# Modulation rows in six groups: one ahead of layer 0, five between its projections, in 32-column strips

## The reference

```python
def _modulation(cond, w, b):
    return jnp.split(jax.nn.silu(cond) @ w + b, N_MOD, axis=-1)      # N_MOD = 6, D = 1024
...
for l in range(DEPTH):                                               # DEPTH = 2
    sh1, sc1, g1, sh2, sc2, g2 = _modulation(c[:, None, :], ada_w[l], ada_b[l])
    csh1, csc1, cg1, csh2, csc2, cg2 = _modulation(c_ctx[None, None, :], ada_w[l], ada_b[l])
    ux = x * (1.0 + sc1) + sh1
    uc = ctx * (1.0 + csc1) + csh1
    yx, yc = _hybrid_mixer(ux, uc, w_in[l], ...)          # input projection first
    x = _layer_norm(DEEPNORM_ALPHA * x + g1 * yx, ...)
    fx = _peer(x * (1.0 + sc2) + sh2, ...)
    x = _layer_norm(DEEPNORM_ALPHA * x + g2 * fx, ...)    # ctx likewise, in layer 0
```

## Time and profile before

| | us |
|---|---|
| median of 3 runs (4849.0 to 4859.0) | 4858.26 |
| the profiled execution's span | 4851.8 |
| prologue, to the first transpose of X | 189.84 |
| of it PE in the 384 modulation matmul records | 166.6 |
| projections of layer 0, from there to the barrier | about 286 |
| PE busy over the span | 4056.9 (84%) |

### The profile page before, as it was taken

One profiled execution on the slowest core, in us unless ns is written; L12 is line 12 of the kernel. 1 busy time (PEld: TensorE's weight loads), 2 busy tenths in 40 slices (PEclk: granted clock), 3 DMA queues, 4 the chain that ended last, 5 costly groups with the idle time before them and its releaser, 6 DMA issues.

```text
span 4851.8 us, 47489 instructions
## 1 busy us (share of the span) xinstructions
PE 4056.9 (84%) x11304; PEld 1920.3 (40%) x11304; DVE 3217.5 (66%) x8492; ACT 843.4 (17%) x2182; POOL 1502.4 (31%) x1349
## 2 busy tenths in 40 slices
PE   8999899687887887887888879989788788788887
PEld 1354675333333333333333324456433333333332
DVE  0220864787777887787787863065588787778776
ACT  0100341111111111111111111023111111111111
POOL 0000010344443443443444430001144344344443
PEclk9999799999999999999999999989899999999999
DMA  9411112999998998998999982122499899899998
GB/s 325 161 52 50 66 63 77 365 416 404 376 417 364 420 414 341 411 418 337 420 418 385 416 334 72 38 98 83 170 411 419 343 414 413 335 418 416 391 412 355
DMA packets 260491, 1484.23 MB, mean 306 GB/s; under 512 B 23943, under 2 KB 48775, under 8 KB 95767
## 3 DMA queue, kind: packets, MB, share of 16 engines
q0 software_dynamic: 184320, 1342.26, 67.3%
q1 hardware_dynamic: 76060, 140.67, 8.5%
HBM read 1476.40 MB, written 2.24 MB: 305 GB/s over the span
## 4 chain that ended last, share of the span: by engine, by line
PE 51%; DVE 26%; issue 15%; DMA 6%; DVEq 2%; ACT 1%; POOL 0%; SPq 0%; POOLq 0%; ACTq 0%
PE ps L723 22%; PE ps L715 6%; DMA arena<-in_updown,arena 5%; PE ps L565 4%; DVE arena L1312 3%; DVE arena L1305 3%; PE ps L522 3%; PE ps L580 3%; PE ps L683 3%; PE ps L585 2%; DVE arena L1275 1%; PE ps L652 1%; DVE arena L1280 1%; DVE arena L1278 1%; PE ps L608 1%
## 5 line engine op out<-in xcount | busy, mean ns | idle before, releaser
L723 PE MATMUL ps<-arena 128*128 128x512 f32 x5120 | 2433.3, 620 | 537.8 <-DVE arena L1305 534.7
L976 POOL DMA_INDIRECT arena<-in_updown,arena x1280 | 1461.4, 1142 | 2225.6 <-PE ps L723 1717.8
L723 PEld LDWEIGHTS ps<-arena 128*128 128x128 f32 x5120 | 938.2, 194 | 2000.5 <-DVE arena L1305 1157.6
L1312 DVE CUSTOM_DVE_ANT_0 arena<-arena 128x1024 bf16<-128x1024 f32 x1280 | 1563.2, 1221 | 173.5 <-DMA arena<-in_updown,arena 107.5
L920 ACT ACTIVATE arena<-arena 128x1 f32<-128x1 f32 x1280 | 252.2, 202 | 2726.3 <-DVE arena L1312 2688.5
L1305 DVE TENSOR_SCALAR arena<-CN,arena 128x128 f32<-128x128 f32 x1280 | 440.9, 344 | 85.6 <-ACT arena L920 46.7
L963 POOL TENSOR_TENSOR arena<-arena 128x256 f32<-128x256 f32 x64 | 40.7, 667 | 1092.9 <-DMA arena<-in_bias 1092.9
L715 PE MATMUL ps<-arena 128*128 (+1 forms) x1280 | 302.4, 391 | 2.3 <-ACT arena L936 2.3
L1237 DVE MAX8 arena<-ps 128x8 f32<-128x128 f32 x80 | 24.0, 299 | 388.4 <-PE ps L715 388.2
L715 PEld LDWEIGHTS ps<-arena 128*128 128x128 f32 x1280 | 252.7, 198 | 68.5 <-issue 32.5
L565 PE MATMUL ps<-arena 128*128 128x512 f32 (+1 forms) x672 | 233.5, 508 | 0.0
(11 more groups left out here) (184 smaller groups left out, 2894.6 us busy)
## 6 DMA issues: line engine op xcount, KB each, us to landing
arena<-in_ada_w SPq DMA_DIRECT2D x24, 2048.0 KB, 7.9
arena<-in_updown,arena POOLq DMA_INDIRECT x1280
arena<-in_wq SPq DMA_DIRECT2D x32, 512.0 KB, 4.3
arena<-in_w_in SPq DMA_DIRECT2D x6, 2048.0 KB, 8.8
arena<-in_w_in SPq DMA_DIRECT2D x24, 512.0 KB, 3.8
arena<-in_bias SPq DMA_DIRECT2D x16, 512.0 KB, 3.6
arena<-in_w_out SPq DMA_DIRECT2D x2, 4096.0 KB, 13.4
arena<-negm_rows SPq DMA_DIRECT2D x16, 384.0 KB, 4.4
```

What stands on the lines that cost most here:

```text
L723: mm = e.matmul(ps[hf][:], diag[:, k % 2, :], ring[:, k % RING, D + hf * 512:D + (hf + 1) * 512], start=False, stop=False, skip_group_chec ...
L976: e.indirect_dma_start(ring[:, k % RING, :], None, updown, bass.IndirectOffsetOnAxis(ap=idx16[:, k:k + 1], axis=0)).then_inc(sem(f"rows{k ...
L1312: e.tensor_tensor_reduce(prod[:, k % 2, :], ring[:, k % RING, 0:D], u, 1.0, 0.0, ALU.mult, ALU.add, dots[:, k:k + 1]).then_inc(sem("L.dot_ ...
```

## The change

The 12288 columns become six groups of 2048. A group is multiplied as four pieces of 512 columns whose results go to partitions 0, 32, 64 and 96 of one PSUM bank: each matmul addresses one 32-column strip of the array (128 rows x 32 columns, strip g). The stationary operand is padded from 2 to 32 columns with zeros (`sT32`). Group 0 (the first 2048 columns of layer 0) is done ahead of layer 0. Groups 1 to 5 are done during the projections of layer 0: after job 17 + 9(g-1) + k PE runs slice k of group g (the four strips for one 128-row block k, 4 matmuls). POOL loads the 1 MB of each slice into one of two buffers, loads the biases, and stores finished rows. DVE adds bias and ones for all four pieces in one 128x512 instruction; four full transposes then give the columns for `modcol`, for layer 0 in the prologue and for layer 1 after group 3. Bank 7 belongs to the groups, so the jobs of layer 0 rotate over 7 banks. The columns and later consumers are otherwise the same.

```diff
+ADA_GROUP = 4 * 512
+ADA_GROUPS = L * N_MOD * D // ADA_GROUP
+ADA_PER_LAYER = ADA_GROUPS // L
+ADA_FIRST_JOB = 17
+ADA_STRIDE = KD + 1
...
+def ada_after_job(n):
+    m = n - ADA_FIRST_JOB
+    group, k = 1 + m // ADA_STRIDE, m % ADA_STRIDE
+    return (group, k) if m >= 0 and group < ADA_GROUPS and k < KD else None
...
-        modcol = sb("modcol", [P, L, N_MOD * KD, 2])
+        modcol = sb("modcol", [P, L, 4, 4, 2])
         sT = sb("sT", [P, KD, 2])
+        sT32 = sb("sT32", [P, KD, 32])
...
-        adaw = r(3, KD, 512)
-        adab = r(L * N_MOD * D)
-        modrow = r(L * N_MOD * D)
+        adaw = r(KD // 2, 2, ADA_GROUP)
+        adab0 = r(512)
+        modrow0 = r(512)
...
+        adak = [Region(proj_top)(ADA_GROUP), Region(ARENA_W - 512 - ADA_GROUP)(ADA_GROUP)]
+        adab1 = Region(ARENA_W - 512)(512)
+        modrow1 = Region(vml_at - 512)(512)
...
+        STORED_GROUPS = [n for n in range(1, ADA_GROUPS) if n % ADA_PER_LAYER]
+        BANKS = [7, 8]
...
-            e.dma_start(adab[0:2, :], ada_b.rearrange("(o l) n -> o (l n)", o=1).to_broadcast([2, L * N_MOD * D])).then_inc(sem("adab_loaded"), 16)
-            for n in range(24):
-                if n >= 3:
-                    e.wait_ge(sem("mod_mm"), n - 2)
-                e.dma_start(adaw[:, n % 3], ada_w[n // 12].rearrange("(k p) n -> p k n", p=P)[:, :, (n % 12) * 512:(n % 12 + 1) * 512]).then_inc(sem(f"adaw_loaded{n % 3}"), 16)
-                if n == 2:
-                    e.dma_start(CN[:], consts[:, 0:C_KEEP]).then_inc(sem("const_loaded"), 16)
-                    e.dma_start(X[:], xin.rearrange("(t p) d -> p t d", p=P)).then_inc(sem("x_loaded"), 16)
-            e.wait_ge(sem("mod_row"), 24)
-            for l in range(L):
-                e.dma_start(mod_d[l], mod_v[0:2, l, :]).then_inc(sem("mod_stored"), 16)
-            e.wait_ge(sem("mod_stored"), 16 * L)
+            for g in range(4):
+                e.dma_start(adab0[32 * g:32 * g + 32, :], bias_of[0, 0, g:g + 1, :].to_broadcast([32, 512])).then_inc(sem("adab0_loaded"), 16)
+            for n in range(KD // 2):
+                e.dma_start(adaw[:, n], ada_w[0].rearrange("(k p) n -> p k n", p=P)[:, 2 * n:2 * n + 2, 0:ADA_GROUP]).then_inc(sem(f"adaw_loaded{n}"), 16)
+            e.dma_start(CN[:], consts[:, 0:C_KEEP]).then_inc(sem("const_loaded"), 16)
+            e.dma_start(X[:], xin.rearrange("(t p) d -> p t d", p=P)).then_inc(sem("x_loaded"), 16)
...
+                if l == 0:
+                    e.wait_ge(sem("mod_stored"), 64 * len(STORED_GROUPS))
...
+            def ada_columns(l, rows):
+                for cb in range(4):
+                    mm = e.transpose(ps[7][:, cb * P:(cb + 1) * P], rows[:, cb * P:(cb + 1) * P], ident)
+                mm.then_inc(sem("modcol_t"), 1)
+            def ada_slice(group, k):
+                m = (group - 1) * KD + k
+                e.wait_ge(sem(f"adak_loaded{m % 2}"), 16 * (m // 2 + 1))
+                if k == 0:
+                    e.wait_ge(sem("mod_row"), group)
+                    e.wait_ge(sem("modcol_kept"), (group - 1) // ADA_PER_LAYER + 1)
+                for g in range(4):
+                    mm = e.matmul(ps[7][32 * g:32 * g + 32, :], sT32[:, k, :], adak[m % 2][:, g * 512:(g + 1) * 512], start=(k == 0), stop=(k == KD - 1))
+                mm.then_inc(sem("adak_mm"), 1)
             e.wait_ge(sem("silu_c"), 1)
-            for n in range(24):
-                e.wait_ge(sem(f"adaw_loaded{n % 3}"), 16 * (n // 3 + 1))
-                if n >= 4:
-                    e.wait_ge(sem("mod_row"), n - 3)
-                for k in range(KD):
-                    mm = e.matmul(ps[n % 4][0:2, :], sT[:, k, :], adaw[:, n % 3, k, :], start=(k == 0), stop=(k == KD - 1))
-                mm.then_inc(sem("mod_mm"), 1)
-            e.wait_ge(sem("mod_row"), 24)
+            for n in range(KD // 2):
+                e.wait_ge(sem(f"adaw_loaded{n}"), 16)
+                for k in range(2):
+                    for g in range(4):
+                        mm = e.matmul(ps[7][32 * g:32 * g + 32, :], sT32[:, 2 * n + k, :], adaw[:, n, k, g * 512:(g + 1) * 512],
+                                      start=(n == 0 and k == 0), stop=(n == KD // 2 - 1 and k == 1))
+            mm.then_inc(sem("mod_mm"), 1)
+            e.wait_ge(sem("mod_row"), 1)
             e.wait_ge(sem("const_loaded"), 16)
-            for l in range(L):
-                for c in range(N_MOD * KD):
-                    mm = e.transpose(ps[4 + l][:, 2 * c:2 * c + 2], mod_v[0:2, l, c * P:(c + 1) * P], ident[0:2, 0:2])
-                mm.then_inc(sem("modcol_t"), 1)
+            ada_columns(0, modrow0)
...
-                    if n >= 8:
-                        w, val = freed[n - 8]
+                    if n >= BANKS[l]:
+                        w, val = freed[n - BANKS[l]]
                         e.wait_ge(sem(f"L.proj_evac_{w}"), val)
                     count[ev] += 1
                     freed.append((ev, count[ev]))
-                    bank = ps[n % 8]
+                    bank = ps[n % BANKS[l]]
...
+                    if l == 0:
+                        if ada_after_job(n):
+                            ada_slice(*ada_after_job(n))
+                        if ada_closed_after(n - 1) == ADA_PER_LAYER:
+                            e.wait_ge(sem("mod_row"), ADA_PER_LAYER + 1)
+                            ada_columns(1, modrow1)
...
+            e.wait_ge(sem("sT32_zero"), 1)
+            e.activation(sT32[:, :, 0:2], sT[:], ACT.Silu).then_inc(sem("silu_c"), 1)
...
+                        if l == 0 and i == NCT - 1:
+                            e.wait_ge(sem("mod_stored"), 64 * len(STORED_GROUPS))
...
+                    for group in range(1, ADA_GROUPS):
+                        al, i = group // ADA_PER_LAYER, group % ADA_PER_LAYER
+                        if group >= 2:
+                            e.wait_ge(sem("mod_row"), group)
+                        for g in range(4):
+                            e.dma_start(adab1[32 * g:32 * g + 32, :], bias_of[al, i, g:g + 1, :].to_broadcast([32, 512])).then_inc(sem("adab1_loaded"), 16)
+                        for k in range(KD):
+                            m = (group - 1) * KD + k
+                            if m >= 2:
+                                e.wait_ge(sem("adak_mm"), m - 1)
+                            e.dma_start(adak[m % 2], ada_w[al, k * P:(k + 1) * P, i * ADA_GROUP:(i + 1) * ADA_GROUP]).then_inc(sem(f"adak_loaded{m % 2}"), 16)
+                        if i:
+                            e.wait_ge(sem("mod_row"), group + 1)
+                            for g in range(4):
+                                e.dma_start(mod_to[al, :, i, g, :], modrow1[32 * g:32 * g + 2, :]).then_inc(sem("mod_stored"), 16)
+                    e.wait_ge(sem("mod_stored"), 64 * len(STORED_GROUPS))
...
-            e.wait_ge(sem("adab_loaded"), 16)
-            for n in range(24):
-                e.wait_ge(sem("mod_mm"), n + 1)
-                one = 1.0 if (n % 12) // 2 in (SC1, SC2) else 0.0
-                e.scalar_tensor_tensor(out=modrow[0:2, n * 512:(n + 1) * 512], in0=ps[n % 4][0:2, :], scalar=one,
-                                       in1=adab[0:2, n * 512:(n + 1) * 512], op0=ALU.add, op1=ALU.add).then_inc(sem("mod_row"), 1)
-            e.wait_ge(sem("modcol_t"), L)
-            for l in range(L):
-                e.tensor_copy(modcol[:, l].rearrange("p a b -> p (a b)"), ps[4 + l][:, 0:2 * N_MOD * KD])
...
+            def ada_row(group, dst, bias_row):
+                i = group % ADA_PER_LAYER
+                if SC1 // 2 == i or SC2 // 2 == i:
+                    one = one_sc1 if SC1 // 2 == i else one_sc2
+                    ins = e.scalar_tensor_tensor(out=dst, in0=ps[7][:], scalar=one[:, 0:1], in1=bias_row, op0=ALU.add, op1=ALU.add)
+                else:
+                    ins = e.tensor_tensor(dst, ps[7][:], bias_row, ALU.add)
+                ins.then_inc(sem("mod_row"), 1)
+            def ada_keep(l):
+                e.wait_ge(sem("modcol_t"), l + 1)
+                e.tensor_copy(modcol[:, l], ps[7][:].rearrange("p (cb g r) -> p g cb r", cb=4, g=4)[:, :, :, 0:2]).then_inc(sem("modcol_kept"), 1)
+            e.wait_ge(sem("adab0_loaded"), 64)
+            e.wait_ge(sem("mod_mm"), 1)
+            ada_row(0, modrow0, adab0)
+            ada_keep(0)
...
+                        group = ada_closed_after(n - 1)
+                        if group is not None:
+                            e.wait_ge(sem("adab1_loaded"), 64 * group)
+                            e.wait_ge(sem("adak_mm"), KD * group)
+                            if group >= 2:
+                                e.wait_ge(sem("mod_stored"), 64 * sum(x < group for x in STORED_GROUPS))
+                            if group == ADA_PER_LAYER + 1:
+                                e.wait_ge(sem("modcol_t"), 2)
+                            ada_row(group, modrow1, adab1)
+                        if ada_closed_after(n - 2) == ADA_PER_LAYER:
```

(39 more changed lines are left out.)

8 lines of the change are left out of this document (7 added, 1 removed).

## The result

The changed kernel takes 4746.06 us (median of 4 runs, 4743.12 to 4754.48) against 4856.27 (4 runs): a ratio of 0.9779, 95% interval 0.9765 to 0.9793. That is 110 us less by the medians and 107 by the ratio. The forecast was 4767, with a range from 4747 to 4806. The direction and the mechanism were right, and the gain was larger than the forecast 91.6 us by 15 to 19 us. The profiled execution fell from 4851.8 to 4745.6 us, 106.2.

A forecast was written before the change was run, and what follows sets the result against it. PE, not the transfers, was taken to bound prologue and projections. Prologue -152.8, slices +56, waits +6, extra transposes +0.5, gates -1.3 sum to -91.6 us: from 4858.3 to 4767 us, range 4747 to 4806.

The forecast's parts named there:

- Part 1, the prologue: Ahead of layer 0: transfers of 12.1 MB set the end, first transpose of X at 37.0 us, 152.8 us saved.
- Part 2, the slices: Layer 0's projections: 40 slices on a busy PE, four strips at once, 1.4 us each, 56 us added.
- Part 3, waits: Layer 0's projections: PE waits for POOL's weight loads, 0 to 27 us, taken as 6 us.
- The short places with an R job: Projections: four or five places with little PE work to cover a slice's load, 0 to 3 us of waiting each.
- The wait for the gates: Projections: PE's 1.3 us wait for the gates goes, since five slices now stand ahead of it.
- the clock: Prologue and transposes of X: half clock costs little, 0, at most 2 us more.
- DVE's adds, the bank and `mod_stored`: Projections up to the barrier: added DVE work, seven banks instead of eight, and waits for stored rows each cost 0.
- The sum: Whole kernel: -152.8 + 56 + 6 + 0.5 - 1.3 = -91.6 us, giving 4767 us.
- The lower bound of 4747: Whole kernel: slices of 1.1 us, no waits, and first transpose of X at 35 us, all together.
- Pairs of strips: Slices: only two strips run at a time, 84 us for the slices, 4792 us in all; chance 0.18.
- Serial strips: Slices and prologue: strips run one after another, slices cost 153.2 us, 4867 us, slower than before; chance 0.16.
- POOL's loads as the pace: Projections: POOL's queue needs 10 us from wait to landing, 43 us of waits, 4804 us; chance 0.06.

The follow-up runs named there:

- Run 6: The changed kernel with the constants and X queued ahead of the bias and the weights: 4745.54 us, ratio 0.9773.
- runs 3 and 5: 3: changed kernel, all six groups in four strips ahead of layer 0, 4810.08 us; 5: kernel before, layer 0's jobs over seven PSUM banks, 4854.04 us.
- run 1: The changed kernel with all four pieces of a slice sent to strip 0 and summed there, in the prologue too: 4848.48 us, ratio 0.9987.
- run 7: The changed kernel, POOL issuing the next group's first two weight loads before the row's wait, stores and bias loads: 4741.36 us, ratio 0.9768.

## Why the prediction was right, step by step

**Part 1, the prologue.** Right: the flow of 12.1 MB sets it, PE and DVE are done before X lands. 34.49 instead of 37.0 us. From 6 to 33 us the DMAs moved 417 GB/s, weights in pieces of 8 KB, where I took 395 from chunks in 2 KB pieces; that is 1.2 us. That the size of the pieces is the cause no run shows. The other 1.3 us are allowances: by that rate the 12.1 MB had flowed by 33.2 us and X was there at 34.24, 1 us later, where I had about two for the slowest engine, and the barrier took 0.25 us and not 0.5. The term was 2.5 us too small in gain. Run 6 shows the bound by moving it.

**Part 2, the slices.** Right in mechanism: all four at once, read from two row halves that ran side by side in the earlier trace rows. The mis-sized term is the slice: 1.19 us, not 1.4. Streaming was 0.86 as taken, and the visit's cost 0.33, where I had 0.4 for two changes of shape and 0.15 for weight loads. The way back costs the 0.2 us of the earlier trace rows: the first full-array record starts 0.095 us late and the second 0.107. The way into the strips is what I had too high, 0.13 us instead of 0.35: 0.095 before their first record and 0.03 between first and second halves, with all weight loads in it, since the four strips load almost together (0.16 us for all eight). The first part of that, 0.095, is about the length of one weight load (0.107), so I probably counted the loads twice; no run separates them. The three slices between G jobs cost 0.86 flat. 56 us became 3 x 0.86 + 37 x 1.19 = 46.6: 9 us, the largest miss.

By an estimate from the Trainium skill's 2.38 times for three column strips ("TensorE: Matmul & The Clock Gate", Part 3) the stream would have been 1.08 us. The runs show 3.43, 1.72 and 0.86 for one, two and four strips, and the measurement decides for full speed on a busy array. The Trainium skill's rule (the same page, Part 3) that weight loads overlap matmuls in flight only when the row group differs does not describe these records either. Eight loads of the same rows lie within 0.16 us of 300.60, and the second four of them start while the strips' first records, from 300.60 to 301.22, are running.

**Part 3, waits.** 3.2 us of waits for loads, not 6. All four waits are for the first or second slice of a group, behind a boundary. The short places with an R job inside a group, where I had up to 3 us each, cost nothing. The rows of PE's waits after, over 34 to 368 us:

```profile
PE ps L603 <- PEq L418: 3.4, 1, 3.4
PE ps L566 <- DMA arena<-in_ada_w: 3.2, 4, 1.2
PE ps L610 <- DVE arena L1164: 0.9, 1, 0.9
```

POOL issues a plain 1 MB load in 0.53 us and a small one in 0.5, not in the 1 us that I took from the gathers:

```profile
95.75 2.03 POOL L1031 DMA_DIRECT2D mod_rows<-arena  x4 [7.51 <-DVE arena L1076]
97.77 2.00 POOL L1022 DMA_DIRECT2D arena<-in_ada_b  x4
99.77 1.09 POOL L1027 DMA_DIRECT2D arena<-in_ada_w  x2
106.56 0.53 POOL L1027 DMA_DIRECT2D arena<-in_ada_w  x1 [5.71 <-PE ps L566]
```

The wait for the gates (1.3 us) went as forecast. Another 1.7 us went that I had not seen: in the trace of before the first M jobs behind that wait ran at a granted clock of 0.50 for 3.4 us. That wait alone does not bring it, since runs 3 and 5 had the same wait and kept 1.00, so these 1.7 us belong to the one trace. I had costed the clock at 0 to 2 us more; it came to some 2 us less, the T jobs' 0.5 with it. The 0.85 us between records that I called half clock there is not in the lines of the earlier trace rows, which begin at a gap of 0.64; it is in the same timeline just ahead of them, with loads at 12.77, 13.62 and 14.48 us. DVE's adds, the bank and `mod_stored` were free, as costed.

**The sum.** Off by 2.5 (start), 9.4 (slices), 2.8 (waits) and 2.2 (clock, T jobs), 17 us together, less 2.3 us of scatter in the rest: 14.6 us between -91.6 and -106.2. All four misses had the same sign. The lower bound of 4747 took the best case of three parts at once, and the median still came out 1 us under it: the start of 34.49 lay under its bound of 35, and the clock had a bound on the slow side alone.

**The rivals.** Pairs of strips would have shown four groups of 0.43 us; the changed kernel shows two, and the first records of all four strips start before any second one (308.658 to .678, then 309.112), so records do not start in the strict order that this rival needs. Serial strips were run 1. POOL's loads as the pace: 3.2 us of waits, and run 7 takes even these away.

## What to carry to other kernels

Two changes that each earn little can be worth much together when one frees the engine and the other hides the transfers: ask of each what bounds the stretch once it is in, and cost the second from there. Work with a stationary operand of at most 32 columns gains from column strips. Each visit to them costs some 0.33 us here, so fewer and longer visits pay while the loads still come in time, and beside jobs that use the same shape a visit is free. On a DMA queue, issue first what an engine waits for, and put stores and small loads behind it: that took away all 3.2 us of PE's waits for loads in run 7. Gains of this size show in the traces and not clearly in the times of whole runs.

## What the runs showed of the hardware

- Float32 matmuls in four 32-column strips streamed at four times the rate of one strip: 3.43, 1.72 and 0.86 us for four 512-column pieces in one, two and four strips, with starts 7 ns apart.
- A visit to the strips from full-array matmuls costs 0.32 to 0.34 us in all, whether one, two or four strips, one slice or two; between 8-column matmuls it costs nothing (three slices, 2.58 us). Of it 0.13 us lie on the way in and 0.20 on the way back.
- Plain loads issued by POOL in the changed kernel cost it 0.53 us per 1 MB in 8 KB pieces, where the indirect ones of the earlier trace rows cost 0.94 and 1.08, and land in 5.3 us (median of 40).
- PE's 48 transposes of X took 5.43 us at a granted clock of 1.00, 6.63 at 0.81, 7.82 at 0.69 and 8.33 at 0.64. An idle 3.3 us before them stood beside 0.79, and so did an idle 0.64 us (table in run 6).
- From 6 to 33 us of the changed kernel's prologue the DMAs moved 417 GB/s, with weights in 8 KB pieces, against 395 from 12 to 34 us of before, with weights in 2 KB pieces. No run changed the size of the pieces alone.
